# Two transformer blocks on one core: the linear-attention values and the closing projection computed with tokens on the partitions

## The reference, cut to what matters

```python
# block one, end
x = x + memory_cross_attention(hx, hm, xa_wq, xa_wkv, xa_wo)   # "x2" below
x = rms_norm(x, final_norm_g)                                   # "x3", the residual of block two
# block two
h = rms_norm_2(x, g_pre)                                        # "h2"
proj = h @ w_in                                                 # split: ..., cq, ck, cv (4 heads x 256), c_gate, c_lr (16 columns), ...
z = (lr @ w_alpha + b_alpha); log_a = log_sigmoid(z) / 16       # decays of the linear attention
kv = einsum('bcjhk,bcjhv->bchkv', kc * exp(b_last - bc), vc)    # per chunk of 64 tokens; v is used token by token
merged = gates[0]*(y_a @ w_br_pool) + gates[1]*(y_b @ w_br_swa) + gates[2]*(y_c @ w_br_gla) + gates[3]*(y_m @ w_br_mem)
x = x + rms_norm_2(merged @ w_out, g_post)
```

## Time and profile before

| | us |
|---|---|
| time, median of 3 runs | 3535.0 (3533.56 to 3536.11) |
| time of the profiled execution | 3533.81 |
| its span, first to last instruction | 3532.0 |
| PE busy | 3398.0 (96%) |
| POOL / ACT / DVE busy | 1387.0 / 1070.2 / 882.9 |
| mean granted PE clock | 0.987 |

### The profile page before, as it was taken

One profiled execution on the slowest core, in us unless ns is written; L12 is line 12 of the kernel. 1 busy time (PEld: TensorE's weight loads), 2 busy tenths in 40 slices (PEclk: granted clock), 3 DMA queues, 4 the chain that ended last, 5 costly groups with the idle time before them and its releaser, 6 DMA issues.

```text
span 3532.0 us, 41492 instructions
## 1 busy us (share of the span) xinstructions
PE 3398.0 (96%) x15617; PEld 2764.0 (78%) x15617; DVE 882.9 (25%) x1494; ACT 1070.2 (30%) x1577; POOL 1387.0 (39%) x601
## 2 busy tenths in 40 slices
PE   6899999999999799999999999999999999999998
PEld 5877878787877477788887877877888887888786
DVE  4275423112123612310022122121111124200313
ACT  5344222223234433322222222232222222222322
POOL 3644232333442243434433333333444434444342
PEclk9999999999999899999999999999999999999998
DMA  6623222332431333333332332323333333333432
GB/s 191 197 61 90 66 78 66 83 83 76 124 110 48 100 84 84 86 87 96 97 88 72 84 83 77 84 77 84 96 96 100 96 101 84 102 96 95 140 95 71
DMA packets 604018, 329.15 MB, mean 93 GB/s; under 512 B 16620, under 2 KB 592372, under 8 KB 602884
## 3 DMA queue, kind: packets, MB, share of 16 engines
q1 hardware_dynamic: 595828, 317.57, 32.3%
q10 hardware_dynamic: 8080, 10.03, 0.9%
HBM read 314.71 MB, written 12.85 MB: 93 GB/s over the span
## 4 chain that ended last, share of the span: by engine, by line
PE 85%; issue 7%; DVE 4%; POOL 2%; ACT 2%; DVEq 0%; ACTq 0%; POOLq 0%
PE proj L617 76%; POOL w_lo L597 2%; PE s L892 2%; PE t L658 1%; PE s L881 1%; PE s L755 0%; DVE w_st L2682 0%; PE s L1229 0%; DVE xy L2834 0%; DVE xy L2833 0%; DVE xy L2497 0%; DVE ht_lo L2091 0%; PE s L991 0%; PE s L617 0%; PE s L1090 0%
## 5 line engine op out<-in xcount | busy, mean ns | idle before, releaser
L597 POOL TENSOR_TENSOR w_lo<-raw,w_hi 128x1024 fp32r<-128x1024 f32 x572 | 1384.9, 2435 | 2094.0 <-ACT w_hi L1259 2073.1
L617 PE MATMUL proj<-ht_hi,w_hi 128*128 128x512 f32 (+1 forms) x4032 | 1569.9, 389 | 16.7 <-DVE ht_lo L2430 6.0
L617 PE MATMUL proj<-ht_hi,w_lo 128*128 128x512 f32 (+1 forms) x4032 | 1546.4, 384 | 0.0
L617 PE MATMUL proj<-ht_lo,w_hi 128*128 128x512 f32 (+1 forms) x4032 | 1545.7, 383 | 0.0
L617 PEld LDWEIGHTS proj<-ht_hi,w_hi 128*128 128x128 f32 x4032 | 760.6, 189 | 177.5 <-issue 22.6
L617 PEld LDWEIGHTS proj<-ht_lo,w_hi 128*128 128x128 f32 x4032 | 760.8, 189 | 151.3 <-issue 7.0
L617 PEld LDWEIGHTS proj<-ht_hi,w_lo 128*128 128x128 f32 x4032 | 760.1, 189 | 150.2
L1259 ACT ACTIVATE w_hi<-raw 128x1024 fp32r<-128x1024 f32 x570 | 584.1, 1053 | 768.0 <-PE proj L617 726.9
L617 PE MATMUL proj<-yh,w_hi 128*128 128x512 f32 x384 | 149.8, 390 | 3.9 <-DVE yl L2450 2.2
L617 PE MATMUL proj<-yl,w_hi 128*128 128x512 f32 x384 | 149.4, 389 | 0.0
L617 PE MATMUL proj<-yh,w_lo 128*128 128x512 f32 x384 | 149.4, 389 | 0.0
(11 more groups left out here) (480 smaller groups left out, 2243.5 us busy)
## 6 DMA issues: line engine op xcount, KB each, us to landing
raw<-in_w_in_dram SPq DMA_DIRECT2D x404, 512.0 KB, 3.8
raw<-in_w_out_dram SPq DMA_DIRECT2D x64, 512.0 KB, 4.0
raw<-in_xa_wkv_dram SPq DMA_DIRECT2D x16, 512.0 KB, 4.5
raw<-in_w_mem_kv_dram SPq DMA_DIRECT2D x16, 512.0 KB, 4.5
raw<-in_w_br_gla_dram SPq DMA_DIRECT2D x16, 512.0 KB, 3.9
raw<-in_w_br_pool_dram SPq DMA_DIRECT2D x16, 512.0 KB, 3.8
mem_tok<-in_mem_dram SPq DMA_DIRECT2D x4, 1024.0 KB, 7.9
x_tok<-in_x_dram SPq DMA_DIRECT2D x1, 4096.0 KB, 15.2
```

What stands on the lines that cost most here:

```text
L597: pool.tensor_tensor(w_lo[:, slot, :], raw[:, slot, :], w_hi[:, slot, :].bitcast(F32), ALU.subtract).then_inc(lo_done, 1)
L617: ins = pe.matmul(dst, w, x[:, kt, c0:c1], start=first and n == 0 and m == 0, stop=last and n == len(kts) - 1 and m == 2)
```

## The change

- **Gate projections.** `mlg` and `glr` leave the ring. Their weights come by one DMA each, ACT and DVE make the hi and lo halves, and these lie side by side in one stationary operand: `narrow` makes 32 passes (`ht_hi` and `ht_lo` against both halves at once) where 48 stood. A selection matrix (`gate_sel`) or doubled rows of `w_alpha` (`g_wh`, two small DMAs a head from ACT) add the halves up.
- **Block two's opening.** `ht_hi`/`ht_lo` first hold u = x2 * g_pre, written during `xwo` (ACT, and `u_low` on DVE). The values of all four heads come from u, tokens on the output partitions: u's 128x128 tile is stationary, 512 weight columns move (`v_rows`, 384 matmuls, eight PSUM banks; sixteen loads of 128 x 1024). Meanwhile PE transposes x2 (`x2_rows`), ACT squares rows with an accumulated sum, DVE writes x3's unnormalised rows, ACT stores them by DMA (`x3_spill`). Row sums give `r`; it scales the values at the banks' draining (`v_kept`), and four matmuls spread it over the partitions (`n_rstd`). h2 is then written in place of u, tile k after the values have used it. The two phase barriers, the spills of x2 and of the root, the value units' copies and transposes go.
- **Heads.** Four units each, written out instead of a loop. The first head's ACT list is logs, exponentials, then `ahead(b, 2)`, `ahead(b, 4)`.
- **Closing projection.** `y2_rows`: merged's tiles stationary, w_out's 512 columns moving, four column blocks over two sets of four banks; in the last one the token tiles finish one after another. ACT squares rows with a sum, DVE scales by `g_post` rows, the residual is read as token rows and scaled earlier; per token tile a root, a reciprocal and two 1024-wide steps, then a 512 KB output DMA for each.

The diff, cut to what the text speaks of:

```diff
-PHASES = [("kv", 32, 16), ("lru", 16, 8), ("mlg", 4, 0), ("ml", 36, 18), ("moba", 48, 24), ("wout", 32, 16),
-          ("xq", 8, 4), ("xwo", 8, 16), ("glr", 4, 0), ("gla", 48, 24), ("merge_g", 48, 32), ("swa", 80, 40),
+PHASES = [("kv", 32, 16), ("lru", 16, 8), ("ml", 36, 18), ("moba", 48, 24), ("wout", 32, 16),
+          ("xq", 8, 4), ("xwo", 8, 16), ("gv", 16, 2), ("gla", 32, 16), ("merge_g", 48, 32), ("swa", 80, 40),
...
-            for q in range(4):
-                half(H4["mlg"], q, w1[512 * q:512 * q + 512, C_ML_I:C_ML_I + 8], n=8, ks=4)
...
+            for kt in range(KT):
+                sp.wait_ge(lo_done, th(H4["gv"], kt) - RING)
+                sp.dma_start(raw[:, kt % RING, :], w2[kt * P:kt * P + P, C_GV:C_GV + HALF]).then_inc(
+                    raw_ready[kt % RING], 16)
...
+            def narrow(dst, w, n, fresh=None):
+                for kt in range(KT):
+                    if fresh is not None:
+                        pe.wait_ge(ht_ready, fresh + kt + 1)
+                    for m, x in enumerate((ht_hi, ht_lo)):
+                        ins = pe.matmul(dst, w[:, kt * n:kt * n + P], x[:, kt, :], start=kt == 0 and m == 0,
+                                        stop=kt == KT - 1 and m == 1)
+                return ins
+            pe.wait_ge(mlg_ready, 1)
+            narrow(S[3][:], mlg_w, 16).then_inc(mlg_done, 1)
...
+            def x2_rows(g):
+                pe.wait_ge(bank_free[0], Q2["xwo"] + 2 * g + 2)
+                pe.wait_ge(bank_free[1], Q2["xwo"] + 2 * g + 2)
+                for t in range(NT):
+                    if g:
+                        pe.wait_ge(x3_kept, 4 * g - 3 + t)
+                    transposes(S[t], [xy[:, 4 * g + n, t * P:(t + 1) * P] for n in range(4)]).then_inc(x2_t, 1)
+            for n in range(2, KT):
+                bank_wait(Q2["xwo"], n)
+                accumulate(H4["xwo"], n // 2, proj[n % 2][:], range(4), n % 2, o_hi, o_lo, (0, T), True, True,
+                           None, done=n % 2 == 1, step=2)
+                if n in (4, 8, 12):
+                    x2_rows(n // 4 - 1)
...
+            def v_rows(blk, t, kts):
+                for kt in kts:
+                    pe.wait_ge(lo_done, th(H4["gv"], kt))
+                    pe.wait_ge(ht_ready, HT_U + kt + 1)
+                    wh, wl = [w[:, kt % RING, blk * T:blk * T + T] for w in (w_hi, w_lo)]
+                    for m, (x, w) in enumerate(((ht_hi, wh), (ht_lo, wh), (ht_hi, wl))):
+                        ins = pe.matmul(VB[blk][t][:], x[:, kt, t * P:(t + 1) * P], w, start=kt == 0 and m == 0,
+                                        stop=kt == KT - 1 and m == 2)
+                    if blk == 1 and t == NT - 1:
+                        ins.then_inc(half_done, 1)
+                return ins
+            v_rows(0, 0, [0])
+            v_rows(0, 1, [0])
+            bank_wait(Q2["gv"], 0)
+            v_rows(0, 2, [0])
+            bank_wait(Q2["gv"], 1)
+            v_rows(0, 3, [0])
+            x2_rows(3)
+            for kt in range(1, 4):
+                for t in range(NT):
+                    v_rows(0, t, [kt])
+            for t in range(2):
+                pe.wait_ge(x3_kept, 13 + t)
+                v_rows(1, t, range(4))
+            pe.wait_ge(x3_kept, 16)
+            pe.wait_ge(r_diag, NT)
+            for t in range(NT):
+                ins = pe.matmul(S[3][:, t * P:(t + 1) * P], ones[:], n_diag[:, t, :], start=True, stop=True)
+            ins.then_inc(r_pe, 1)
+            v_rows(1, 2, range(4))
+            pe.wait_ge(r_kept, 1)
+            v_rows(1, 3, range(4))
+            for kt in range(4, KT - 2):
+                for blk in range(2):
+                    for t in range(NT):
+                        v_rows(blk, t, [kt])
+            for blk in range(2):
+                for t in range(NT):
+                    ins = v_rows(blk, t, [KT - 2, KT - 1])
+                    if blk == 0 or t < NT - 1:
+                        ins.then_inc(gv_done, 1)
...
+            def low_rank():
+                pe.wait_ge(lr_ready, 1)
+                pe.wait_ge(gv_act, 2)
+                narrow(TB[1][:], lr_w, 32, HT_H2).then_inc(glr_done, 1)
...
+                b, qb = H4["gla"] + 2 * i, Q2["gla"] + 2 * i
+                if i:
+                    unit(b, 0, qb, 0)
                     gla_o(i - 1)
+                else:
+                    unit(b, 0, qb, 0, fresh=HT_H2, among=low_rank)
+                    pe.wait_ge(gv_dve, 2)
+                    pe.wait_ge(glr_kept, 1)
+                    gla_z(0)
                 unit(b, 2, qb, 1)
-                if before:
+                if i:
                     gla_out(i - 1)
-                pe.wait_ge(gla_wh, i + 1)
-                pe.matmul(S[0][:], g_wh[:], g_lr[:], start=True, stop=True).then_inc(gla_pe.sem, 1)
-                taken(qb, 0)
-                transposes(TB[1], blocks(g_v)).then_inc(gla_pe.sem, 1)
-                unit(b, 4, qb, 2)
-                taken(qb, 1)
-                transposes(TB[0], blocks(g_v)).then_inc(gla_pe.sem, 1)
-                unit(b, 6, qb, 3)
-                unit(b, 8, qb, 4, among=(lambda: gla_scores(i)) if last else None)
+                unit(b, 4, qb, 2, among=(lambda: gla_scores(i)) if last else None)
...
+            for fb in range(4):
+                if fb == 1:
+                    bank_wait(Q2["wout2"], 0)
+                    bank_wait(Q2["wout2"], 1)
+                elif fb > 1:
+                    pe.wait_ge(y2_act, 4 * fb - 4)
+                    pe.wait_ge(y2_dve, 4 * fb - 4)
+                for kp in range(8 if fb < 3 else 4):
+                    if fb == 0:
+                        pe.wait_ge(ht_ready, HT_MERGED + 2 * kp + 2)
+                    for t in range(NT):
+                        y2_rows(fb, t, kp)
+            for t in range(NT):
+                for kp in range(4, 8):
+                    y2_rows(3, t, kp)
...
+            def x2_square(g, t):
+                act.wait_ge(x2_t, 4 * g + t + 1)
+                need(act, x2_sq, 4 * g + t)
+                act.activation(n_t0[:], S[t][:], ACT.Square, accum_out=n_ss[:, 4 * t + g:4 * t + g + 1]).then_inc(x2_sq, 1)
+            def x3_square(g, t):
+                act.wait_ge(x3_kept, 4 * g + t + 1)
+                need(act, x2_sq3, 4 * g + t)
+                k = 16 + 4 * t + g
+                act.activation(n_t1[:], x3u[:, t, :], ACT.Square, accum_out=n_ss[:, k:k + 1]).then_inc(x2_sq3, 1)
...
+            def x3_store(g):
+                act.wait_ge(x3_kept, 4 * g + 4)
+                act.dma_start(x3_spill[:, g * T:g * T + T].rearrange("(t p) d -> p t d", p=P), x3u[:]).then_inc(x3_out, 16)
...
+            act.wait_ge(x2_ms, 1)
+            act.activation(small[:, 40:48], small[:, 40:48], ACT.Sqrt).then_inc(x2_root, 1)
+            act.wait_ge(lr_in, 16)
+            act.activation(lr_w[:, 0:KT * 32].rearrange("p (k n) -> p k n", n=32)[:, :, 0:16], lr_raw[:], ACT.Copy
+                           ).then_inc(lr_hi, 1)
+            def wh_load(i):
+                for r in range(2):
+                    act.dma_start(g_wh[16 * r:16 * r + 16, :], a["w_alpha_2"][0][:, i * P:(i + 1) * P]).then_inc(gla_wh, 16)
+            wh_load(0)
+            act.wait_ge(r_pe, 1)
+            act.activation(n_rstd[:], S[3][:], ACT.Copy).then_inc(r_kept, 1)
+            def v_kept(blk):
+                for t in range(2):
+                    act.wait_ge(gv_done, 4 * blk + t + 1)
+                    act.activation(g_vt[:, t, blk * T:blk * T + T], VB[blk][t][:], ACT.Copy, scale=r_h2[:, t:t + 1]
+                                   ).then_inc(gv_act, 1)
+            for k in range(KT):
+                ahead(H4["gv"], k + 2, 1)
+                if k == KT - 2:
+                    v_kept(0)
+                act.wait_ge(norm_t, KT + k + 1)
+                act.activation(ht_hi[:, k, :], nt["t"][k % 2][:], ACT.Copy).then_inc(norm_hi, 1)
...
+                    gla_logs(0)
+                    gla_exps(0)
+                    ahead(b, 2)
+                    ahead(b, 4)
...
+            def x3_rows(g, t):
+                dve.wait_ge(x2_sq, 4 * g + t + 1)
+                if g and t == 0:
+                    dve.wait_ge(x3_out, 16 * g)
+                    dve.wait_ge(x2_sq3, 4 * g)
+                dve.tensor_tensor(x3u[:, t, :], S[t][:], gf_row[:, g * T:g * T + T], MUL).then_inc(x3_kept, 1)
+            def u_low(k):
+                dve.wait_ge(norm_hi, HT_U - KT + k + 1)
+                dve.scalar_tensor_tensor(ht_lo[:, k, :], xy[:, k, :], col("g_pre", k), ht_hi[:, k, :].bitcast(F32),
+                                         MUL, SUB).then_inc(ht_ready, 1)
+            for n in range(KT):
+                g, s = (n - 5) // 4, (n - 5) % 4
+                if n >= 5 and s < 2:
+                    x3_rows(g, 2 * s)
+                    x3_rows(g, 2 * s + 1)
+                if n % 2:
+                    unit_in(H4["xwo"], n // 2)
+                else:
+                    dve.wait_ge(part_done, n // 2 + 1)
```

(48 more changed lines are left out.)

535 lines of the change are left out of this document (265 added, 270 removed).

## The result

| | before | after |
|---|---|---|
| median of the runs shown, us | 3534.55 (3533.56 to 3536.11, 4 runs) | 3471.59 (3470.05 to 3476.24, 4 runs) |
| profiled execution, span in us | 3532.0 | 3469.3 |
| ratio after / before | | 0.9824, 95% interval 0.9807 to 0.9841 |

What follows compares the result with a forecast made beforehand. PE, busy 96% of the span, was taken as the bound. Gains of 29.6, 3.7, 28.1 and 2.4 less 0.5 at the start sum to 63.3 us, giving a forecast of 3470 in the range 3457 to 3487.

Steps and rivals of the forecast that it cites:

- Work in part one: Output projection to end of linear attention: PE's work alone, without waits, takes 370.0 us after the change.
- Waits in part one: Output projection to end of linear attention: PE's remaining waits, 10.2 us in all including 3.2 for slow passes.
- The ring: Weight slots in the values: fifth half's copy and w_lo start late, so PE waits 1.6 us once.
- The first head: Linear attention: ACT's weight copies stand behind logs, exponentials and three table loads, so PE waits 4.6 us.
- The wait in `xwo`: Output projection: tile 10's add stands behind two x3_rows, themselves behind ACT's squares; PE waits 0.8 us.
- Clock: Output projection to end of linear attention: two spells of slow passes after waits, 1.6 us each, 3.2 together.
- `xwo` and the collisions: Output projection, rival: u_low steps meeting w_lo hold up adds and PE's banks, +16 us, 3486; chance 0.17.
- The norm: Before r is spread: chain behind tile 15 is covered by PE's passes, wait 0, with 1.3 us to spare.
- Closing projection, end, gates: Gains of 3.7 us in the closing projection, 28.1 after the last matmul, 2.4 from 16 fewer gate passes.
- The start: Kernel's opening: one early DMA of 2048 small pieces goes ahead of the first weights, costing 0.5 us, between 0 and 3.
- Operands in their new role: Rival: 1152 passes with weights moving and activations stationary run slower, 3700 at the lower level; chance 0.03.
- No waits at all: Rival, better case: the forecast waits of 10.2 us and 1.2 at the gates vanish, 3459; chance 0.11.

Runs made afterwards that it cites:

- combined kernel: Kernel after with first half's weight copy before first-head logarithms, small loads behind the logarithm, yl behind key steps, last ring turn's value tiles by turns: 3458.9 us, 0.9786 of before.
- run with DVE loaded: Kernel after with three unused copies of u_low added on DVE at every second tile of the output projection: 3484.5 us.
- early exponential: Kernel after with one exponential on a single column put ahead of the first head's logarithms, where ACT is idle: 3467.1 us.
- closing projection at the old pace: Kernel after with the closing projection's first column block computed token tile by token tile, four weight halves at a time: 3474.9 us.
- after again: The kernel after, unchanged, run a second time beside a later variant on the same chip: 3470.5 us.

## Why the forecast held, step by step

- *Work in part one.* 370.0 forecast. The combined kernel takes 369.5 from `xwo` tile 2 to the last transposes, with 0.5 of waits and no slow pass: 369.0. `x2_rows` took 6.6 (4 x 1.66) where I had 7.6, the `xwo` tiles 38.9 where I had 40.3; the rest of the list is 1.4 over, which I did not take apart.
- *Waits in part one.* 7.0 forecast without the clock (0.8, 1.6, 4.6), 7.1 measured (1.79, 3.26, 2.06), but not the same ones. The ring was right (1.6, measured 1.79). The first head was 1.3 too long, because I put the third table load behind DVE's decay; the row at 1290.95 begins right behind the logarithm and ends while ACT still waits 1.49 for DVE. The wait in `xwo` did not come. The wait in the last head I missed: I costed all heads by one, and did not ask what the last one does differently.
- *Clock.* 3.2 forecast as two spells. 380.9 - 369.0 - 7.1 leaves 4.8 in part one: 2.8 behind the first head, 1.6 behind the last head, the rest in the restart behind each wait. And 1.5 more came in the merge, where the change does nothing (last section), with 0.5 elsewhere: the -2.0 of the table. How much of this an execution gets was not to be forecast from the rows; that it came to 6.3 and not more is luck.
- *`xwo` and the collisions.* Result right, reason wrong. I had written that 5 us of 13.4 are free for them. The run with DVE loaded shows that they are not: 25.5 us of DVE's time cost 14 of PE's. It does not show the rival's own price (16 for 16): its groups come in pieces of 2.3 to 4.4, the rival's would be of 2.0 each, and that was not run. The rival stayed away because `u_low` was hardly ever held up: 14 of its 16 steps took 0.74 to 0.75, two, which began in the middle of a `w_lo`, took 1.63 and 2.05. Two of the 14 met a `w_lo` as well, but began before it, and then POOL's step took 2.9 to 3.0 instead of 2.4:

```profile
1151.29 0.74 DVE L2674 SCALAR_TENSOR_TENSOR ht_lo<-xy,par,ht_hi 128x512 fp32r<-128x512 f32 x1
```

```profile
1151.33 2.96 POOL L612 TENSOR_TENSOR w_lo<-raw,w_hi 128x1024 fp32r<-128x1024 f32 x1 [4.01 <-ACT w_hi L1361]
```

  What decided was where the steps fell, by as little as 0.04.
- *The norm.* Right that nothing waits; the margin was 3.5, not 1.3.
- *Closing projection, end, gates.* 3.7, 28.1 and 2.4 forecast; 4.0, 28.5 and 3.0 measured. At the gates the wait behind them was 1.44 as forecast (1.3), and a wait of 0.5 one step further went too, which I had not read. The start was priced at -0.5; no cost shows, within a spread of 2.0 from one profile to another. Together start and gates were 1.5 better than forecast, the largest miss in the table after the -2.0.
- *The other rivals.* Operands in their new role: 0.227 a pass, excluded. No waits at all: the combined kernel shows that 3459 was there to be had, but by other orders than this change's.
- *Rules of the Trainium skill.* By the Trainium skill ("ScalarE: Activation LUTs", section "Table sets: the hidden batching unit") exponential and logarithm share a load; here they don't, in after (loads at 1286.96, 1288.91 and 1290.95) and with the early exponential, and one load less in the chain shortened the wait by 1.3. That page's other statement there, that identity and absolute value are in every set, the same run bears out for the set it had loaded: no load stands before them. By the Trainium skill ("GPSIMD Engine Reference", section "Specifications") POOL's SBUF interfaces are contended for by DVE's instructions with two SBUF inputs or in a 2-port perf mode; the trace agrees for the two inputs: `yl` takes 1.5 to 2.9 against 0.69, and two `x3_rows`, one input in PSUM, take 1.47 together in the middle of a `w_lo`, as these rows of DVE and of POOL in the kernel after show:

```profile
1145.44 1.47 DVE L2669 TENSOR_TENSOR x3u<-s,gf_row 128x512 f32<-128x512 f32 x2 [1.65 <-ACT n_t L1805]
```

```profile
1144.91 2.41 POOL L612 TENSOR_TENSOR w_lo<-raw,w_hi 128x1024 fp32r<-128x1024 f32 x1 [4.88 <-ACT w_hi L1361]
```

Errors of 1 to 2 us on both sides cancelled. The sum is 0.6 off; its terms are not that good. The mechanisms of the large terms (fewer passes, no waits for the norms, a short end) were right, the closeness is in part luck.

## What to carry to other kernels

When the bound engine never waits on average, list what is different in the first and the last turn of each loop: two of the three new waits were there, and both were a matter of order on an engine that is idle two thirds of the time. An engine's free time is not a cushion if its list puts the urgent step behind the slow one; load it on purpose once, and see when the bound engine notices. And a helper engine's step that is slow because it meets another's need not be made faster: put behind the urgent step it still took 3.4 a pair here, and nobody waited.

## What the hardware showed that was not expected

- The stretches of slow passes (0.43 apart instead of 0.23) come and go with the same instructions and the same wait ahead of them. The clearest place is one that no edit reaches: at the wait of 2.42 with which the cross attention's query projection begins, the kernel after and the run with the closing projection at the old pace have the same program up to there, and one runs on at the upper clock while the other has 1.5 of slow passes (five of the twelve profiles that share this program have them at this wait). At the wait of 2.2 in the merge behind the memory heads (untouched by the change, before at 2452.83, after at 2421.20) the kernel before has none, the kernel after has 1.5 us of them, and all other profiles but one have 1.5 to 1.7. Behind the wait of 3.3 in the first head they cost 2.8, 2.7, 1.6, 1.6, 2.9, 1.5, 2.8 and 0 in eight executions; behind the wait of 2.1 in the last head 1.6 in five executions and 0 in five. After and after again have the same stretches slow. So a difference of 1 to 4 us between two profiles of different orders can be nothing but this. In the four profiles where the first head's wait was 0.45 or gone, nothing there was slow.

After, then the closing projection at the old pace:

```profile
1042.56 0.47 PE L633 MATMUL proj<-ht_hi,w_hi 128*128 128x512 f32 x1 [2.42 <-DVE ht_lo L2603]
```

```profile
1042.51 0.76 PE L633 MATMUL proj<-ht_hi,w_hi 128*128 128x512 f32 x1 [2.42 <-DVE ht_lo L2608]
```

- A table load does not wait for its activation's input: it started at 1290.95, 2.8 ahead of the exponential that needs it.
- Issuing two small loads from ACT between two activations of a chain costs the chain 0.86.
- What causes or spares the slow passes behind a given wait was not tried and stays open.
